# Two moves in an issue order: the last gate product of head 3 and the last chunk's exponentials

## The reference, cut to what matters

```python
proj = rmsnorm(x) @ w_in                      # columns u | q | k | v | g | low rank
a = pool_mixer(u)       # 4 groups: windowed mean minus self, then @ w_pool[group], * pool_scale
o, S = gla_chunked(q, k, v, logf, S0)         # gated linear attention, 4 heads
b = o * rsqrt(mean(o * o) + EPS) * gla_norm_g * silu(g)
x = x + concat([a, b]) @ w_out
x = x + hier_moe(rmsnorm(x))                  # 16 experts, two for each token
y = rmsnorm(x)
```

## Time and profile before

| what | value |
|---|---|
| median of 3 runs | 885.25 us |
| lowest, highest | 884.42, 887.79 us |
| the profiled execution, its own time | 887.31 us |
| its span in the trace | 885.4 us |
| mean granted TensorE clock | 0.974 |
| PE busy | 844.3 us of the span (95%) |
| DVE, ACT, POOL busy | 521.4, 373.9, 247.2 us |

### The profile page before, as it was taken

How to read it: one execution, slowest core, us unless ns; L and a number is a source line. 1 busy time by engine, 2 the same in 40 slices (tenths; PEclk the granted TensorE clock), 3 DMA queues, 4 the chain that set the end, 5 groups by cost and what they waited for, 6 DMA issues and landing times.

```text
span 885.4 us, 15660 instructions
## 1 busy us (share of the span) xinstructions
PE 844.3 (95%) x5784; PEld 750.6 (85%) x5784; DVE 521.4 (59%) x1202; ACT 373.9 (42%) x706; POOL 247.2 (28%) x273
## 2 busy tenths in 40 slices
PE   4999999999999999998699999999999999999993
PEld 3999879999988887886599998899999999999992
DVE  6527423656778435645585676666666656766661
ACT  7445303545366524543334443344443444333441
POOL 1000000000000110001135555556535546455471
PEclk9999999999999899998599999999999999999997
DMA  9221001101222182535178889888889887799871
GB/s 301 53 96 27 22 1 48 48 1 55 48 96 95 35 296 72 198 149 178 61 233 304 292 295 354 274 301 307 287 308 333 305 289 271 284 364 311 285 235 36
DMA packets 116569, 167.07 MB, mean 189 GB/s; under 512 B 14949, under 2 KB 93865, under 8 KB 116534
## 3 DMA queue, kind: packets, MB, share of 16 engines
q1 hardware_dynamic: 101173, 135.99, 45.2%
q0 software_dynamic: 15360, 30.59, 9.9%
HBM read 147.36 MB, written 41.17 MB: 213 GB/s over the span
## 4 chain that ended last, share of the span: by engine, by line
PE 48%; DVE 1%; ACT 1%; issue 1%; another core or an unknown queue 1%; POOL 0%; POOLq 0%; ACTq 0%; DVEq 0%
PE bank L1807 30%; PE bank L1817 4%; PE bank L1828 3%; PE bank L1819 3%; PE bank L1818 3%; PE bank L1795 2%; PE bank L88 1%; PE bank L1788 1%; ACT split L1910 1%; DVE wdlo L2026 1%; POOL out L1710 0%; PE bank L1800 0%; PE bank L1834 0%; DVE x L2110 0%
## 5 line engine op out<-in xcount | busy, mean ns | idle before, releaser
L1807 PE MATMUL bank<-big,ring 128*128 128x160 f32 x2048 | 284.5, 300 | 0.1
L1807 PEld LDWEIGHTS bank<-big,ring 128*128 128x128 f32 x2048 | 280.3, 190 | 1.4 <-ACT big L1895 0.2
L2026 DVE TENSOR_TENSOR wdlo<-wdn,split 128x1024 fp32r<-128x1024 f32 x64 | 76.7, 1219 | 0.0
L1726 POOL TENSOR_TENSOR hold_at<-ident 128x1 f32<-128x1 f32 x63 | 22.7, 360 | 169.4 <-DVE lists L1964 116.7
L500 PE MATMUL bank<-split,ring_r 128*128 128x384 f32 (+1 forms) x192 | 64.3, 335 | 2.0 <-ACT uT L698 2.0
L1906 ACT ACTIVATE sg<-bank 128x160 f32<-128x160 f32 x64 | 19.5, 304 | 108.1 <-PE bank L1807 99.5
L1910 ACT CAST split<-wdn 128x1024 fp32r<-128x1024 f32 x64 | 64.9, 1039 | 0.0
L502 PE MATMUL bank<-split,ring_r 128*128 128x384 f32 (+1 forms) x192 | 61.7, 321 | 0.0
L1697 POOL DMA_INDIRECT big<-h_rows,lists x32 | 57.4, 1793 | 12.0 <-issue 11.9
L2021 DVE TENSOR_TENSOR hs<-hid,hs 128x128 fp32r<-128x128 f32 x64 | 18.9, 295 | 56.8 <-ACT hs L1912 53.3
L1817 PE MATMUL bank<-split,hs 128*128 128x512 f32 x128 | 52.3, 409 | 0.0
(11 more groups left out here) (375 smaller groups left out, 1784.2 us busy)
## 6 DMA issues: line engine op xcount, KB each, us to landing
wdn<-in_w_down SPq DMA_DIRECT2D x32, 1024.0 KB
ring<-in_w_gate SPq DMA_DIRECT2D x32, 1024.0 KB, 5.8
ring<-in_w_up SPq DMA_DIRECT2D x32, 1024.0 KB
ring<-in_w_in SPq DMA_DIRECT2D x8, 1024.0 KB, 6.2
x<-in_x_prompt SPq DMA_DIRECT2D x8, 512.0 KB, 6.1
h_rows<-h SPq DMA_DIRECT2D x8, 512.0 KB, 2.6
sums<-x SPq DMA_DIRECT2D x8, 512.0 KB, 3.6
v<-in_x_prompt SPq DMA_DIRECT2D x4, 512.0 KB, 6.7
```

The source lines that it names most:

```text
L1807: x = nc.tensor.matmul(bank[f % 2][:, side * 256:side * 256 + W], ring[:, u, k, c0:c0 + P], xT[:, k, :], start=k == 0, stop=k == KC - 1)
L2026: nc.vector.tensor_tensor(wdlo[:, k, :], wdn[:, k // 2, (k % 2) * D:(k % 2 + 1) * D], wdhi[:, k, :].bitcast(F32), ALU.subtract).then_inc(e ...
```

## The change: what it does

```diff
--- before.py
+++ after.py
@@ -293,7 +293,7 @@
                 [[("g", 3, 0)], [("g", 0, 1)], [("g", 1, 1)]],
                 [[("g", 2, 1)], [("g", 3, 1)], mix[0]],
                 [mix[1], [("g", 0, 2)], [("g", 1, 2)]],
-                [mix[2] + [("g", 2, 2)], [("g", 3, 2)] + mix[3], []]]
+                [[("g", 2, 2)] + mix[2], [("g", 3, 2)] + mix[3], []]]
     groups += [g for chunk in between for part in chunk for g in part]
     index = {g: n for n, g in enumerate(groups)}
     ON_ACT = {"lr", "k", "q", "u", "mix"}
@@ -817,6 +817,8 @@
         for c in range(TT - 1):
             fill(c, 0)
+            if c == TT - 2:
+                exps(TT - 1)
             keys_rows(c)
@@ -833,7 +835,7 @@
             if c == 3:
                 state_rows()
-            if c + 2 < TT:
+            if c + 2 < TT - 1:
                 exps(c + 2)
```

## The result

The changed kernel took 890.12 us (median of 12 runs, 888.59 to 896.14) against 885.69 us for the kernel before, measured beside it (12 runs, 884.42 to 888.17). The ratio is 1.0054, with a 95% interval of 1.0038 to 1.0070: slower by 3.4 to 6.2 us. A second series gave 1.0060 (1.0038 to 1.0081). The profiled execution has a span of 890.3 us and its own time of 892.08 us; granted clock 0.968 in the mean, against 0.974.

A forecast was written before the change was run, and what follows sets the result against it. TensorE, busy 95% of the span, was taken to bound the kernel. Scores +2.1 us (exponentials' gain included) and clock +1.5 made +3.6 us on 885.25: 888.8 us, range 885.5 to 892.0.

The forecast's parts named there:

- Exponentials, minus 0.61: Before ("g", 0, 2), ScalarE's copies start sooner, so TensorE's wait shrinks from 0.68 to 0.07 us: minus 0.61 us.
- Rival D: Late exponentials delay decayed_k(8) beyond its cover and hold chunk 7; the 0.6 gain is lost, +4.2 us, 889.4 us; chance 0.06.
- Who is waited for: Mix 2's third group waits for VectorE's copy of ("g", 2, 2), queued behind out_norm(7) and four gate products, ending at 281.75.
- Rival C: VectorE's copy is not what TensorE waits for; bank rotation removes both old waits, -2.0 us, 883.3 us; chance 0.04.
- The stand, 4.2 us, and +2.1 us for the scores: TensorE stands about 4.2 us before mix 2's third group; scores of chunk 8 start 2.1 us later than before.
- Nothing absorbs it: From scores of chunk 8 to the projection everything moves by 2.1 us; TensorE's own queue stays last, by 1.7 us.
- The clock behind the stand, +1.5: TensorE's clock falls during or right after the stand; dense work runs at half speed about 3 us: plus 1.5 us.
- My own sign: Expected evidence in the profile: a granted clock of 0.50 for 2 to 4 us from about 281 on.
- rival A: Clock stays down longer after the stand, 6.6 us, slowing nearly all of ("g", 3, 2): +5.4 us, 890.7 us; chance 0.17.
- The second fall, no change: The clock's fall at 289.4, at narrow matmuls L585, recurs at unchanged cost; bounds -1.9 and +1.9 us.

The follow-up runs named there:

- the copy first: Changed kernel with VectorE's copy of ("g", 2, 2) moved before the norm of chunk 7 and the gate products; 885.38 and 886.21 us, ratios 0.9993 and 0.9987.
- the filled stand: Changed kernel plus 26 dense products, results unread, on TensorE between the second and third group of mix 2; 889.65 and 888.8 us, ratios 1.0035 and 1.0033.
- the list alone: Kernel before with only ("g", 2, 2) moved in front of mix 2's third group, exponentials left in place; 891.75 us, ratio 1.0071.
- one gate ahead: Changed kernel with VectorE's copy of ("g", 2, 2) placed after one of the four gate products; ratio 0.9993.

## Why the prediction was right, and which term was small

Forecast were 888.8 us, +3.6 us, range 885.5 to 892.0; measured 890.12, +4.4 us, in the range. Step by step:

- **Exponentials, minus 0.61.** Right to the hundredth. The first product of ("g", 0, 2) started with no wait, ScalarE's next step not later than before. VectorE waited 0.45 us for them at `decayed_k(8)`, and the idle time of 1.07 us in front of `decayed_q(8)` was used up to nothing. Rival D, that this cover fails, did not happen: the kernel with the exponentials alone has mix 3 the whole 0.61 sooner.
- **Who is waited for.** Right: VectorE's copy of ("g", 2, 2), behind the norm and the gates. The kernel with the copy first shows it by moving that copy alone. Rival C, the rule on banks, did not happen: here three banks in rotation hid the copy when it stood in front of the norm and the gates, and not when it stood behind their 4.3 us.
- **The stand, 4.2 us, and +2.1 us for the scores.** Measured 4.18; the filled stand, where the clock holds, has the scores 2.21 us late. In the changed kernel they are 2.85 us late, as the third group ahead of them already ran at half clock.
- **Nothing absorbs it.** Right. The projection started 4.43 us late, the next block 4.99. VectorE's last step before the projection ended at 295.57, TensorE's own queue at 296.73, so TensorE was still last, by 1.2 us where it had been 1.7.
- **The clock behind the stand, +1.5.** The fall came as forecast, in the last 0.7 us of the stand, but the term was mis-sized: it measured 2.8 (4.99 - 2.20). I had read the 2.9 us from 293.1 to 296.0 as the time that dense work takes to bring the clock back. It was the end of a slow stretch of 6.8 us as a whole, and the one at the stand was as long, 6.8 us, although ("g", 3, 2) is dense from 283.7 on. My own sign, a clock of 0.50 for 2 to 4 us from about 281 on, failed with it. This was rival A's case in length: 6.1 us of it on work, 2.8 us lost, for which A had 3.3. I gave it 0.17; three of the three profiles with a stand of 4.2 us (the changed kernel twice, the list alone) showed it. Why it stayed down that long is not shown.
- **The second fall, no change.** Right in sum. The prediction's 2.8 us from the turn to L585 to the fall is a misreading: they count from 286.6, where L575 begins, and L585 began at 287.64, so the fall, at about 289.2, came 1.5 us into it; no term rests on this. In the changed kernel it came 2.2 us into L585 instead of 1.5 and lasted 6.8 us as before, so it cost 0.56 us less there (+4.43 at the projection) and 0.56 us more in the projection (+4.99 behind it).

2.1 and 2.8 are 4.9, and the two profiles show 4.99 and 5.12. The medians show 4.4 and 4.8. The chances said same within 0.5% at 0.70 and slower at 0.28; the ratio of 1.0054 lies just beyond the line between them, with an interval to both sides. With the clock term at its measured size the forecast would have been 890.2. That the forecast missed by no more than 0.8 us of change is in part luck: the profiles moved by 1.4 us more than it said, and the median of the first series by half a microsecond less than the profiles.

## What to carry to other kernels

When groups rotate through a few banks, moving a group changes which copy, on which engine, the group behind it waits for: look up that copy's place in the other engine's own order before moving anything. Here both waits had been chosen away correctly and a third one, with a queue of 4.3 us in front of a copy of 0.5 us, cost more than both. Together with the copy the move wins 2 us at mix 3 in the profile; that it wins device time is not shown. And price a new stand of the matmul engine with the slow clock behind it: in the profiles here that was 2.8 us on top of 2.2.

## What the runs showed of the hardware that I had not expected

- A stand of 2.44 us between dense groups was followed by a fall of the granted clock from 1.00 to 0.50, 1.7 us after work had resumed; one of 1.57 us was not. There is one profile of each.
- The slow stretches came in few lengths: 3.4 us after stands of 2.4 and 3.3 us, 6.8 us after 4.2 us. The one at the samples' narrow products was 6.8 us in nine profiles and 3.4 us in three, both of the kernel with the copy first and the one with one gate ahead; there the next block began 3.6 and 1.8 us sooner than before, though mix 3 had won only 2.05 and 0.41. In eleven of the twelve profiles the fall came 1.5 to 3.4 us into L585, in the one with one gate ahead 4.1 us after L585 began, when the projection was already running. The stretches of the kernel with the copy first:

```profile
284.00:288.00 4.00, 4.00 (x33) 3.52 (x31) 4.00 (x8) 3.95 (x8) 0.00 (x0) 1.00 0.02 4
288.00:292.00 4.00, 4.00 (x17) 3.49 (x17) 3.10 (x5) 3.27 (x5) 0.00 (x0) 0.59 0.00 0
292.00:296.00 4.00, 4.00 (x19) 3.26 (x18) 0.61 (x2) 0.00 (x0) 0.00 (x0) 0.99 0.00 0
```

- The spread of one kernel's time goes with the granted clock. In the 17 runs of the kernel before beside the last two kernels, those at a mean of 0.973 or more took 884.35 to 886.12 us, with one of 889.18; those at 0.971 and 0.972 took 886.87 to 888.09. Which is the cause of the other these runs do not say. A gain of 2 us, like that of the copy first, is within what this moves.
